# PE's additions of gathered rows, two gathers later in its order

## The reference

```python
def peer_mixer(h, w_q, sub_keys, u, v):
    ...
    # 8 heads x 16 best of 128 x 128 experts for each token: 128 experts
    def chunk(args):
        hh, ii, gg = args
        a = jnp.einsum('tkd,td->tk', u[ii], hh)
        w = gg * jax.nn.gelu(a)
        return jnp.einsum('tk,tkd->td', w, v[ii])
    ...
# per layer:
    x = x + peer_mixer(rmsnorm(x, ffn_norm[i]), peer_wq[i], peer_keys[i], peer_u[i], peer_v[i])
    g = jax.nn.sigmoid((rmsnorm(x, ple_norm[i]) @ ple_wg[i]).astype(jnp.float32)).astype(x.dtype)
    x = x + g * (p[i] @ ple_wp[i])
```

## Time and profile before

| | |
|---|---|
| median of 3 runs | 2883.5 us |
| profiled execution | 2884.08 us |
| its span | 2882.3 us |
| busy: PE | 2265.8 us, 79% |
| busy: DVE | 2143.5 us, 74% |
| busy: POOL | 1282.7 us, 45% |
| busy: ACT | 1072.4 us, 37% |
| software DMA queue (gathers) | 1073.81 MB, 90.3% of 16 engines |
| hardware DMA queue (weights) | 98.24 MB, 8.4% |

### The profile page before, as it was taken

The page is one execution under the profiler, slowest core; times in us unless marked ns, Lnnn a source line. Parts: engine busy times, 40 slices in busy tenths (PEclk is TensorE's granted clock), DMA queues, the critical chain, the costliest instruction groups (busy, mean ns, idle before and its releaser), DMA issues.

```text
span 2882.3 us, 23329 instructions
## 1 busy us (share of the span) xinstructions
PE 2265.8 (79%) x6572; PEld 1170.4 (41%) x6572; DVE 2143.5 (74%) x4489; ACT 1072.4 (37%) x3181; POOL 1282.7 (45%) x1029
## 2 busy tenths in 40 slices
PE   6787667976978987888687898799967788666555
PEld 4444234522534553455253455346624433222112
DVE  6888768875797667757979766686696977677776
ACT  2443324333334333632323434364332334333222
POOL 2353543544434544533543443454444334555552
PEclk9899988988999998999898999999988999887877
DMA  9999999999999999999999999999999999999995
GB/s 363 420 399 420 419 421 401 417 420 420 419 408 412 380 420 420 419 420 420 408 420 384 416 374 419 421 419 420 420 398 420 419 420 420 420 420 420 420 421 216
DMA packets 164786, 1175.37 MB, mean 408 GB/s; under 512 B 18480, under 2 KB 19888, under 8 KB 23600
## 3 DMA queue, kind: packets, MB, share of 16 engines
q0 software_dynamic: 147456, 1073.81, 90.3%
q1 hardware_dynamic: 16624, 98.24, 8.4%
q10 hardware_dynamic: 576, 1.84, 0.2%
HBM read 1171.71 MB, written 2.10 MB: 407 GB/s over the span
## 4 chain that ended last, share of the span: by engine, by line
PE 36%; DMA 35%; DVE 18%; ACT 5%; issue 4%; POOL 2%; DVEq 0%; SPq 0%; ACTq 0%; POOLq 0%
DMA slot<-in_uv,idx 35%; PE acc L933 18%; DVE slot L1648 6%; DVE X L1639 3%; PE B L687 3%; PE B L605 3%; PE M L605 2%; POOL slot L582 2%; PE M L875 2%; PE M L687 1%; PE B L875 1%; ACT diag L1158 1%; DVE SD L1275 1%; DVE top_u L1280 1%; ACT A L948 1%
## 5 line engine op out<-in xcount | busy, mean ns | idle before, releaser
L933 PE MATMUL acc<-slot,diag 128*128 128x512 f32 x2904 | 1550.7, 673 | 580.9 <-ACT diag L1158 580.1
L582 POOL DMA_INDIRECT slot<-in_uv,idx x1024 | 1282.4, 1252 | 1555.3 <-PE acc L933 1076.4
L1648 DVE CUSTOM_DVE_ANT_0 slot<-slot,HP 128x1024 f32<-128x1024 f32 x1024 | 1243.3, 1221 | 564.2 <-DMA slot<-in_uv,idx 554.4
L933 PEld LDWEIGHTS acc<-slot,diag 128*128 128x128 f32 x2904 | 571.5, 210 | 1413.0 <-ACT diag L1158 853.7
L1150 ACT ACTIVATE act_a<-a 128x1 f32<-128x1 f32 x1024 | 206.6, 202 | 1616.7 <-DVE a L1648 1615.7
L1639 DVE SCALAR_TENSOR_TENSOR X<-slot,w,X 128x1024 f32<-128x1024 f32 x297 | 380.7, 1282 | 33.4 <-ACT w L1152 33.2
L1152 ACT ACTIVATE w<-act_a,gate 128x1 f32<-128x1 f32 x1024 | 301.5, 294 | 33.2
L1158 ACT ACTIVATE diag<-cst,w 128x128 f32<-128x128 f32 x726 | 291.7, 402 | 23.8
L687 PE MATMUL B<-TT,w 128*128 128x256 f32 (+1 forms) x448 | 88.8, 354 | 0.0
L687 PE MATMUL M<-TT,w 128*128 128x256 f32 (+1 forms) x448 | 88.3, 352 | 0.0
L687 PEld LDWEIGHTS B<-TT,w 128*128 128x128 f32 x448 | 78.3, 196 | 20.7 <-issue 13.1
(11 more groups left out here) (203 smaller groups left out, 1553.5 us busy)
## 6 DMA issues: line engine op xcount, KB each, us to landing
w<-in_wq SPq DMA_DIRECT2D x28, 1024.0 KB, 9.1
slot<-in_uv,idx POOLq DMA_INDIRECT x1024, 16.9
w<-in_ple_wg SPq DMA_DIRECT2D x8, 1024.0 KB, 9.1
w<-in_w_o SPq DMA_DIRECT2D x8, 1024.0 KB, 9.1
w<-in_w_dq SPq DMA_DIRECT2D x6, 1024.0 KB, 6.9
w<-in_w_uq_nope SPq DMA_DIRECT2D x8, 768.0 KB, 8.6
w<-in_ple_wp SPq DMA_DIRECT2D x5, 1024.0 KB, 14.2
slot<-in_wq SPq DMA_DIRECT2D x4, 1024.0 KB, 15.2
```

The lines of the kernel that those rows point to most:

```text
L582: nc.gpsimd.indirect_dma_start(out=slot[s][:], out_offset=None, in_=uv[g // NC], in_offset=bass.IndirectOffsetOnAxis(ap=idx[:, g % HPB, k: ...
L933: last = nc.tensor.matmul(acc[:, half * 512:half * 512 + 512], diag[adds_on_pe(n) % DIAGS][:], slot[s][:, D + half * 512:D + half * 512 + ...
L1648: nc.vector.tensor_tensor_reduce(out=slot[s][:, 0:D], in0=slot[s][:, 0:D], in1=HP[:, g % HPB, :], scale=1.0, scalar=0.0, op0=ALU.mult, op1 ...
```

## The change

Only PE's queue changes. Its `gather(n)` no longer issues the addition of gather `n`; it puts `n` in a list and issues the oldest one of it when more than `PE_BEHIND` = 2 are held. Since `run_between` runs the stage steps of a gather ahead of `gather(n)`, the addition of `n` now stands behind the steps placed at `n + 1` and `n + 2`. At the end of a pair, `close_pair` issues those still held. What an addition waits for and what it tells are unchanged. An entry that DVE adds is held and dropped like the others, without an instruction.

```diff
 DVE_HEAD = 3
+PE_BEHIND = 2
...
+            held = []
+
             def gather(n):
+                held.append(n)
+                if len(held) > PE_BEHIND:
+                    add_row(held.pop(0))
+
+            def close_pair(g):
+                while held:
+                    add_row(held.pop(0))
+
+            def add_row(n):
                 if on_dve(n):
                     return
                 g, k = divmod(n, KSEL)
...
             pe.wait_ge(cst_loaded, 16)
-            run_between(stages, gather)
+            run_between(stages, gather, close_pair)
```

## The result

The changed kernel takes **2896.16 us** (median of 5 runs, 2894.72 to 2899.46) against 2883.5 us (5 runs, 2882.57 to 2885.29): ratio 1.0044 with the interval [1.0033, 1.0055], 12.7 us slower. The forecast was 2881 us; the time lies on the rival of the slots and 0.16 us above the end of the range. The profile after, from its page: span, rate by slice, chain of waits, POOL's issues.

The account below looks back on a forecast made before the run. The prediction took DMA transfers at 420 GB/s plus lost transfer time as the bound. Its terms, +2 + 1 - 6 + 0 = -3 us, gave about 2881 us as a median, range 2869 to 2896.

Parts of the forecast that it names:

- the rival of the slots: Whole kernel: slot time decides, nine slots work like seven wherever a step waits for DVE or ACT; 2896 us, chance 0.24.
- What bounds the kernel: Whole span: transfers alone take 2798.5 of 2882.3 us; 39.0 us of lost transfer time in the middle could be won.
- Everything else: 0 us: Pair 0, pair 1's dense part and the attention parts: no net change, bounds -5 and +5 us.
- Pair 4's and pair 2's embedding, +2 and +1: At 1544 to 1578 and 828 to 848: later additions cost +2 us (-1.7 to +5.2) and +1 us (0 to +5.2).
- Keys and values, -3 each: Pairs 2 and 4: DVE gains 4.2 us on PE's steps, against a later slot; -3 us each, -6 in all.
- signs of the mechanism: Keys and values: SD waits about 2.2 instead of 3.9 us, L1460's wait gone, POOL's issue well under 9, rate above 320.
- signs of the slots: Signs the forecast is wrong: a rate below 300 at 1544 to 1600, or new dips in pair 0 and pair 1.
- Slower, 2896 us: Delayed slots outlast the queue: pair 4's gates cost 5, pair 2's 1, keys and values +3 each; about +12, chance 0.24.
- Slower through ACT: PE's ring of five diags: two more open ones could stop ACT at a diag; 2892 us, chance 0.06.
- Faster, 2870: Keys and values: DVE's waits for PE cause the bursts, losses of 8.1 and 8.3 go almost wholly; -14 us, chance 0.30.

## Why the prediction was wrong

**What bounds the kernel.** Right: the time is transfer time lost, and the account by windows (+12.4) closes with the spans (+12.1).

**The step that failed is "Everything else: 0 us", with bounds of -5 and +5.** It is +14.1 us by the windows: pair 0 +2.3, pair 1 +5.8, attention of pair 5 +9.0, its end -3.0. Done alone the pairs 0 and 1 cost 5.2 us and the attention parts 4.3. The term had no sum behind it. I took a rate of 420 GB/s for room, and PE busy throughout for a sign that additions and steps only change places. The first doesn't hold anywhere: a hold in attention costs, and one slot less costs 12.4 us. The second fails in pair 1, where PE stands 4.58 us at a transposition with a ready addition behind it. In pair 5's attention PE is still busy throughout, and the slots come late all the same, behind steps that are ready; how much of its +9.0 is the hold and how much the low clock from 1942 on is not separated.

**Pair 4's and pair 2's embedding, +2 and +1.** Too small: +5.7 and +3.2 in the whole kernel, together 13.1 us in the run that holds only there. That this run as a whole came to +4.0 is no support for the +3, since 9.0 us of it were won back in keys and values. I had worked out the delay with a transposition that starts when T is free; in the trace the first one waits 4.26 us for A, which isn't written yet, and the second 2.82 us for T.

**Keys and values, -3 each.** The windows give -5.5 and -5.1, but the hold done there alone -0.6 [-3.2, +2.0], and on top of the other places about -3.7, which two overlapping intervals leave uncertain. The signs of the mechanism came as named: SD waits at most 2.6 us instead of 3.9, the wait at the transposition of SD is gone from the waits, POOL's longest issue in the stretch is 6.11 us instead of 9.07, and the rates are above 320. But the time from issue to landing, said to get shorter in all four stretches, does so in two: 7.7 us for 11.4 at 828 to 848 and 9.3 for 10.4 at 922 to 956, against 7.5 for 7.0 at 1544 to 1578 and 10.9 for 8.7 at 1656 to 1690. And the signs of the slots came: 278 GB/s at 1544 to 1578, where "a little below 342" was named, and the new dip of pair 1. Without a hold in the embedding the late slot takes most of the gain back. The prediction also laid the 9.07 us to a DVE instruction that holds POOL until its own end; such a hold gives at most 2.0 us in the trace of before, and why this one lasts for seven instructions is open.

**The rivals.** *Slower, 2896 us*, has the time to the microsecond, and that is luck. Its idea, nine slots that don't suffice, is borne out by the runs with eight slots and with one, two and three held. Its terms are not: it gave keys and values +3 each, which were -5.5 and -5.1, and it left out the attention and had the dip of pair 1 only as a sign. *Slower through ACT* falls: the waits of after hold none of ACT's diag for acc. *Faster, 2870* falls as to the time; but DVE's burst is a loss of its own, and a break in it wins 4.9 us.

**What stays open.** Why a disturbed embedding lessens the loss in keys and values (DVE may come to them with another number of landed gathers) is argued, not tried. How much of pair 5's +9.0 in the profiled run is the hold, how much PE's low clock, and how much a shift from the pair's end (-3.0) is not separated; the hold there alone cost 4.3 us in pairs 3 and 5 together. And what lets two gather issues of 1024 wait for a whole burst of DVE is not known.

## What to carry to other kernels

In an engine that works in order, work that frees buffers, moved behind a step, is late by how long that step takes and by what it waits for. So list for each moved-ahead step both its length and when its input is ready. A full transfer rate says nothing of the room behind it. To learn that, take one buffer away and time the kernel, and time a small dose of the change first: here a hold of one gather won 3.7 us where two lost 12.7. And when windows at fixed times are compared, look whether the dip is still inside.

## What was not expected of the hardware

With one-input maxima put into DVE's burst, POOL's gather issue ended 0.87 us after they began (5.63 us instead of 9.07), and 1.8 us of useless DVE work in each of two pairs made the kernel 4.9 us faster. The price of holding slots grows with each gather in this kernel: the first -3.7 us, the second +16.4, the third +26.5. PE's granted clock fell to 0.50 at 1942 to 1948 us behind 1.79 us of idle time, and the two additions there took 5.81 instead of 3.70 us.
